# A hybrid decoder layer on one core: a new timetable for the mixer blocks, gates in two PSUM banks, an output projection begun early, and fewer query weight loads

## What is computed

```python
x <- LN1(alpha*x + Mixer(x)); x <- LN2(alpha*x + PEER(x))
Mixer: one input projection (1024 -> 2048), then
  group A (512): conv of 4 taps -> RG-LRU (two sigmoid gates, scan) -> * gelu(gate)
  group B (256): y = B * conv of 3 taps (C * x_sc)
  group C (256): softmax attention into 256 memory tokens (4 heads)
  RMSNorm of each group, then one output projection (1024 -> 1024)
PEER: q = x @ wq (16 sides of 128); scores against 128 keys a side; top 16 of the pair sums
  for each of 8 heads; for these 16 experts e of a head:
  out += softmax(score) * gelu(x . u[e]) * v[e]
```

## Time and profile before

| | |
|---|---|
| median of 3 runs | 3273.26 us (3269.31 to 3274.66) |
| the profiled execution | 3269.15 us |
| its span, first to last instruction | 3267.3 us |
| PE busy | 2525.7 us (77%) |
| DVE busy | 2146.8 us (66%) |
| ACT busy | 1432.7 us (44%) |
| POOL busy | 1235.9 us (38%) |
| moved by DMA | 1265.55 MB, mean 387 GB/s |
| of it the gathers (queue q0) | 1140.92 MB |
| granted clock of PE, mean | 0.844 |

### The profile page before, as it was taken

The page is one execution under the profiler, slowest core; times in us unless marked ns, Lnnn a source line. Parts: engine busy times, 40 slices in busy tenths (PEclk is TensorE's granted clock), DMA queues, the critical chain, the costliest instruction groups (busy, mean ns, idle before and its releaser), DMA issues.

```text
span 3267.3 us, 36242 instructions
## 1 busy us (share of the span) xinstructions
PE 2525.7 (77%) x10228; PEld 741.7 (23%) x10228; DVE 2146.8 (66%) x4901; ACT 1432.7 (44%) x4042; POOL 1235.9 (38%) x1092
## 2 busy tenths in 40 slices
PE   8889988789787898677887878876676766666675
PEld 4443432222111232122331112321111111110010
DVE  3545767878766567777767666556666666764554
ACT  3415545566434434456544334434444343443343
POOL 0014433344444344444334444343434343443342
PEclk9989998889898899799887988997767677777677
DMA  3449999899999999999989999999999999999997
GB/s 140 164 187 402 420 417 410 321 365 412 420 420 421 416 420 420 407 399 378 405 335 411 420 420 420 417 416 421 421 411 416 418 412 420 411 419 421 411 413 321
DMA packets 199720, 1265.55 MB, mean 387 GB/s; under 512 B 24160, under 2 KB 27488, under 8 KB 59616
## 3 DMA queue, kind: packets, MB, share of 16 engines
q0 software_dynamic: 156672, 1140.92, 85.1%
q1 hardware_dynamic: 42848, 122.32, 9.9%
HBM read 1245.49 MB, written 17.66 MB: 387 GB/s over the span
## 4 chain that ended last, share of the span: by engine, by line
issue 55%; POOL 33%; DMA 6%; PE 2%; DVE 2%; ACT 1%; POOLq 0%; SPq 0%; DVEq 0%; ACTq 0%
POOL arena L671 33%; DMA arena<-in_uv,idxT 5%; DVE arena L1525 1%; PE ps L940 1%; PE ps L698 1%; POOLq L663 0%; PE ps L720 0%; PE ps L924 0%; DMA arena<-in_w_in 0%; PE ps L889 0%; DVE bst L1485 0%; ACT wt L1130 0%; ACT wset L1135 0%; DVE bst L1383 0%; DVE arena L1393 0%
## 5 line engine op out<-in xcount | busy, mean ns | idle before, releaser
L671 POOL DMA_INDIRECT arena<-in_uv,idxT x1088 | 1235.7, 1136 | 2001.1 <-PE ps L940 1727.6
L940 PE MATMUL ps<-arena,wset 128*32 128x512 f32 x4352 | 1403.9, 746 | 659.4 <-ACT wset L1135 601.2
L1525 DVE CUSTOM_DVE_ANT_0 arena<-arena 128x1024 f32<-128x1024 f32 x1088 | 1329.9, 1224 | 838.8 <-DMA arena<-in_uv,idxT 798.6
L1126 ACT ACTIVATE gel<-acts 128x1 f32<-128x1 f32 x1088 | 219.8, 202 | 1403.8 <-DVE acts L1525 1402.1
L940 PEld LDWEIGHTS ps<-arena,wset 128*32 128x32 f32 x4352 | 176.9, 119 | 1600.2 <-ACT wset L1135 1394.1
L1130 ACT ACTIVATE wt<-gel,gT 128x1 f32<-128x1 f32 x1088 | 320.5, 295 | 102.5 <-ACT gel L1126 2.6
L1135 ACT ACTIVATE wset<-arena,wt 128x32 f32<-128x32 f32 x1088 | 349.5, 321 | 36.0
L698 PE MATMUL ps<-arena 128*128 128x384 f32 (+1 forms) x768 | 311.0, 524 | 28.7 <-DMA arena<-in_w_in 15.2
L859 PE MATMUL ps<-arena 128*128 128x128 f32 (+3 forms) x1024 | 294.8, 420 | 9.4 <-DMA arena<-in_wq 7.8
L924 PE MATMUL ps<-arena 32*128 32x512 f32 x704 | 243.8, 774 | 0.2 <-ACT arena L1108 0.2
L859 PEld LDWEIGHTS ps<-arena 128*128 128x128 f32 x1024 | 164.8, 194 | 208.4 <-issue 171.8
(11 more groups left out here) (171 smaller groups left out, 1514.1 us busy)
## 6 DMA issues: line engine op xcount, KB each, us to landing
arena<-in_wq SPq DMA_DIRECT2D x64, 512.0 KB
arena<-in_w_in SPq DMA_DIRECT2D x48, 512.0 KB
arena<-in_uv,idxT POOLq DMA_INDIRECT x1088
arena<-in_w_outs SPq DMA_DIRECT2D x16, 512.0 KB
arena<-scratch_q SPq DMA_DIRECT2D x30, 256.0 KB
arena<-in_x_tok SPq DMA_DIRECT2D x9, 512.0 KB, 8.1
scratch_x<-arena SPq DMA_DIRECT2D x9, 512.0 KB
arena<-in_w_out SPq DMA_DIRECT2D x1, 4096.0 KB, 13.6
```

What stands on the lines that cost most here:

```text
L671: pool.indirect_dma_start(out=ring[n % RING], out_offset=None, in_=A["uv"], in_offset=bass.IndirectOffsetOnAxis(ap=idxT[t % 2][:, col:col ...
L940: last = mm(ps[r0:r0 + 32, hf * HALF:(hf + 1) * HALF], wset[n % SETS][:, :], v[:, hf * HALF:(hf + 1) * HALF], start=first, stop=final)
L1126: A_(gel[:, n % COLS:n % COLS + 1], acts[:, n % COLS:n % COLS + 1], ACT.Gelu).then_inc(gelus, 1)
L1525: V.tensor_tensor_reduce(out=ring[n % RING][:, 0:D], in0=ring[n % RING][:, 0:D], in1=xrep[g % 2], scale=1.0, scalar=0.0, op0=ALU.mult, op1 ...
```

## The change

- BASE goes from [-200, 76, 384] to [-200, 72, 368]. In blocks 1 and 2 the order of input projections mixes groups A and B (`PROJ1`), a gate starts every 24 steps instead of 16 (`x = o + 16 + 24 * c`), both sigmoids stand on one step, "ra" is split in "ra" and "rc", attention rounds start at o + 18 + 16 r instead of o + 15 + 16 r, norms are spread, and the output projection starts at o + 140 (block 2: o + 150) instead of o + 142.
- Block 2's cache loads: "ss" and "sv" stand 8 steps apart instead of 1 or 3.
- In blocks 1 and 2 "gr" goes to the bank of the projection lx, "gi" to that of lg (`gbank`); norms' banks by `nbank`.
- Head: attention rounds every 3.5 steps instead of 4, the norm of G_MEM at 29 instead of 34, of G_LRU at 27 instead of 28. The two output halves of tile 0 are each split in "oa" (the 6 row blocks of G_LRU and G_MEM, which doesn't wait for G_SC; step 33) and "ob" (the other two; step 36).
- Sides 8 to 15 of block 0 are computed once for all 384 columns ("wa", steps 9 to 41, ACT copies tile 0's part to `qTb` and the rest to the store buffer); "wq" has only sides 0 to 7 left, from step 42. The order of the stores is k = 2, 3, 0, 1.
- First loads: xT is loaded in two halves with a semaphore each, before par and consts on SP; the first three weights, memT and wkv are issued by ACT.

```diff
-BASE = [LEAD, 76, 384]
+BASE = [LEAD, 72, 368]
+PROJ0 = [("qp", 0), ("qp", 1)] + LRU + SC
+PROJ1 = [("qp", 0), ("qp", 1)] + [x for c in range(3) for x in (LRU[2 * c], LRU[2 * c + 1], SC[c])] + LRU[6:] + SC[3:]
+PROJ = [PROJ0, PROJ1, PROJ1]
...
-        put("act", o + 8 * i + 6, b, name, c)
+        put("act", o + 8 * i + (6 if i < 14 else 7), b, name, c)
     for c in range(CL):
-        x = o + 16 * c
-        put("dve", x + 25, b, "cv", c)
-        put("pe", x + 31, b, "gr", c)
-        put("act", x + 31, b, "sr", c)
-        put("pe", x + 31.5, b, "gi", c)
-        put("act", x + 32, b, "si", c)
-        put("act", x + 33, b, "ta", c)
-        put("dve", x + 34, b, "ra", c)
-        put("act", x + 39, b, "sd", c)
-        put("dve", x + 40, b, "re", c)
-    for i in range(CS):
-        put("dve", o + 104.5 + 24 * i, b, "sh", i)
+        x = o + 16 + 24 * c
+        put("dve", x + 9, b, "cv", c)
+        put("pe", x + 15, b, "gr", c)
+        put("act", x + 15, b, "sr", c)
+        put("pe", x + 15, b, "gi", c)
+        put("act", x + 15, b, "si", c)
+        put("act", x + 16, b, "ta", c)
+        put("dve", x + 17, b, "ra", c)
+        put("dve", x + 20, b, "rc", c)
+        put("act", x + 23, b, "sd", c)
+        put("dve", x + 24, b, "re", c)
+    put("dve", o + 89, b, "sh", 0)
+    put("dve", o + 128, b, "sh", 1)
...
-        x = o + 15 + 16 * r
+        x = o + 18 + 16 * r
...
-            put("pe", o + 78 + i + 2 * (i // 2), b, "ss", i)
-            put("pe", o + 98 + i + 2 * (i // 2), b, "sv", i)
-        put("act", o + 85, b, "cs")
-        put("pe", o + 89, b, "sr4")
-        attend(ROUNDS[b], o + 89)
+            put("pe", o + 78 + 8 * i, b, "ss", i)
+            put("pe", o + 114 + 8 * i, b, "sv", i)
+        put("act", o + 104, b, "cs")
+        put("pe", o + 106, b, "sr4")
+        attend(ROUNDS[b], o + 106)
...
-    for g, x in ((G_LRU, 95), (G_MEM, 106), (G_SC, 134)):
+    for g, at, no in ((G_LRU, 115.5, 119), (G_MEM, 118 if b == 1 else 142, 124 if b == 1 else 145), (G_SC, 133, 136)):
...
-        x = 8 + 4 * r
+        x = 7 + 3.5 * r
...
-    for g, x in ((G_LRU, 28), (G_MEM, 34), (G_SC, 35)):
+    for g, x in ((G_LRU, 27), (G_MEM, 29), (G_SC, 35)):
...
-    for n, (ti, half) in enumerate(((0, 0), (0, 1), (1, 0))):
-        put("pe", v(36 + n), "op", (ti, half))
+    for arg in ((0, 0), (0, 1)):
+        put("pe", v(33), "oa", arg)
+        put("pe", v(36), "ob", arg)
+    put("pe", v(38), "op", (1, 0))
...
     for side in range(8, SIDES):
-        put("pe", 9 + 2 * (side - 8), "w0", side)
-        put("act", 9 + 2 * (side - 8) + 2, "w0", side)
-    plan_queries(0, 26, 3)
+        put("pe", 9 + 4 * (side - 8), "wa", side)
+        put("act", 9 + 4 * (side - 8) + 4, "wa", side)
+        if side % 4 == 3:
+            put("sp", 9 + 4 * (side - 8) + 5, "sq", side // 4)
+    plan_queries(0, 42, 3)
...
+    def pbank(b, name, c):
+        return MB[PROJ[b].index((name, c)) % 2]
+    def gbank(b, name, c):
+        return MB[1] if b == 0 else pbank(b, "lx" if name == "gr" else "lg", c)
+    def nbank(b, g):
+        return MB[1] if g == G_LRU or (b and g == G_SC) else MB[2]
+    def q_order(b, k):
+        return (k + 2) % 4 if b == 0 else k
...
-                load("xT", x8(zone1, b), A["xT"][:, :, t0:t0 + n_])
+                for i in range(2):
+                    ks = slice(i * KD // 2, (i + 1) * KD // 2)
+                    load(f"xT{i}", x8(zone1, b)[:, ks, :], A["xT"][:, ks, t0:t0 + n_])
...
+        mix(LEAD - 1)
+        load("par", par[:, :], A["par"])
         load("consts", consts[:, :], A["consts"])
-        load("par", par[:, :], A["par"])
-        mix(LEAD - 1)
-        load("memT", memT, A["memT"])
-        load("wkv", wkv, A["wkv"])
...
-                o_ = claim(MB[(2 * ti + half) % 3], "dve", b, "z", arg)
-                for k in range(KD):
+                ks = GROUPS[G_LRU][1] + GROUPS[G_MEM][1] + GROUPS[G_SC][1]
+                ks = {"op": ks, "oa": ks[:6], "ob": ks[6:]}[name]
+                k_ = MB[(2 * ti + half) % 3]
+                o_ = bank[k_] if name == "ob" else claim(k_, "dve", b, "z", arg)
+                if name == "oa":
+                    pe.wait_ge(ld["wout"], 16)
+                    after(pe, "dve", b, "no", G_LRU)
+                    after(pe, "dve", b, "no", G_MEM)
+                else:
+                    after(pe, "dve", b, "no", G_SC)
...
+        for i in range(WIN):
+            act.dma_start(win[i], A["w_in"][W_COL[PROJ0[i]]]).then_inc(ld_win[i], 16)
+        act.dma_start(memT, A["memT"]).then_inc(ld["memT"], 16)
+        act.dma_start(wkv, A["wkv"]).then_inc(ld["wkv"], 16)
```

More of the change, by code:

```diff
@@ L495, in parts, with last_query @@
         return buf[:, 0:halo + n_], s_
+    def pbank(b, name, c):
[6 more added lines that the diff above has]
+        return (k + 2) % 4 if b == 0 else k
     def q_stores(b, k):
         per_unit = [1, 1, 2]
-        before = sum(per_unit[b_] * 2 for b_ in range(b)) + per_unit[b] * (k // 2)
+        before = sum(per_unit[b_] * 2 for b_ in range(b)) + per_unit[b] * (q_order(b, k) // 2)
         return 16 * (before + per_unit[b])
+    def last_query(b):
+        return "wq", (SIDES // 2 if b == 0 else SIDES) - 1
     def quad(t, c):
@@ L605, in run @@
                 k, s_ = arg, stg[arg % 2]
-                after(sp, "act", b, "we", 4 * k + 3)
+                after(sp, "act", b, "wa" if b == 0 and k >= 2 else "we", 4 * k + 3)
                 t0, n_ = ((1, 2), (3, 3), (6, 2))[b]
@@ L801, in run @@
             elif name == "nm":
-                o_ = claim(MB[0 if arg == G_MEM else 1], "act", b, "rm", arg)
+                o_ = claim(nbank(b, arg), "act", b, "rm", arg)
                 ks = GROUPS[arg][1]
@@ L877, in keyscores @@
             if u < 4:
-                after(pe, "act", 0, "w0", 4 * u + 3)
+                after(pe, "act", 0, "w0" if u < 2 else "wa", 4 * u + 3)
             else:
@@ L974, in past_block @@
                 after(act, "dve", b - 1, "no", g)
-            for k in (2, 3):
-                act.wait_ge(st_q[k % 2], q_stores(b - 1, k))
+            for k in range(4):
+                if q_order(b - 1, k) >= 2:
+                    act.wait_ge(st_q[k % 2], q_stores(b - 1, k))
         def run(b, name, arg):
             n_, n0 = cols(b), BLOCKS[b][1]
-            bk = bank[MB[PROJ.index((name, arg)) % 2]] if (name, arg) in PROJ else None
-            if bk is not None:
+            if (name, arg) in IS_PROJ:
+                bk = bank[pbank(b, name, arg)]
                 after(act, "pe", b, name, arg)
@@ L1054, in run @@
                 after(act, "pe", b, "nm", arg)
-                ins = A_(rmsbuf[arg][:, 0:n_], bank[MB[0 if arg == G_MEM else 1]][:, 0:n_], ACT.Sqrt,
+                ins = A_(rmsbuf[arg][:, 0:n_], bank[nbank(b, arg)][:, 0:n_], ACT.Sqrt,
                          scale=1.0 / GROUPS[arg][2], bias=eps[:, 0:1])
@@ L1372, in run @@
                 if b == 0:
-                    after(dve, "pe", b, "op", arg)
+                    after(dve, "pe", b, "ob" if ti == 0 else "op", arg)
                 else:
```

121 lines of the change are left out of this document (63 added, 58 removed).

## The result

The changed kernel takes 3243.82 us (median of 4, 3243.0 to 3247.56) beside 3272.07 us for the kernel before on the same chip: a ratio of 0.9917, 95% interval 0.9901 to 0.9932. It is faster by 28 us, half of the 57 us forecast. Its profiled execution has a span of 3242.1 us (before: 3267.3).

The account below looks back on a forecast made before the run. The prediction took the kernel to be bound by its DMAs, above all the gathers, at 420 GB/s. Head -4, queries -7, SP wait +2, blocks -23 and -25 sum to -57 us: 3216 us, own range 3198 to 3234, outer 3191 to 3250.

Parts of the forecast that it names:

- The start: Head, first loads on two queues: consts lands after 3.5 MB, PE starts at 12.2 instead of 10.43 us, +1.8 us.
- the upper bound: Head's start: all 6.2 MB issued on ACT and SP there land before consts, first matmul at 19.5 us, +9.1 us.
- rival A: Head: ACT's loads go first, the start is 9.1 us late instead of 1.8; +7.3, total 3223 us; chance 0.27.
- The stretch between: Head, first matmul to last input projection: G_MEM's norm sum (1.5 us) moves ahead of that projection; no other cost.
- the cover: Head: G_LRU and G_MEM normed by the last projection's end, rounds packed for it; if not, up to 5.9 us lost.
- The output projection: Head, tile 0, last projection to transposes: 27.3 instead of 34.7 us, 7.4 less; with the norm sum's 1.5, 5.9 gained.
- Behind the transposes: Head, transposes to first gather: nothing changes, four first query sides and three outputs as before.
- Queries: Block 0, 255 to 461 us: sides 8 to 15's weights loaded once, 4.19 MB less; -7 us, between -3 and -10.
- The new wait on SP: Block 0: tile 1's query loads wait for late stores, PE may wait near step 80; +2 us, from 0 to +10.
- Blocks 1 and 2: Their gather stretches: spaced gates, rounds and cache loads recover bandwidth; -23 us (-10 to -31) and -25 (-12 to -33).
- Rival B: Blocks 1 and 2: losses come from in-order hand-overs, spacing halves them; -12 and -19, total 3233 to 3250; chance 0.20.
- Rival C: Blocks 1 and 2: PE's granted clock falls and PE becomes the bound; at 0.72 the kernel takes 3311 us; chance 0.05.

Follow-up runs that it names:

- e1: The changed kernel with consts and par issued ahead of xT on SP, ACT still issuing its loads: 3250.29 us, ratio 0.9922 to the kernel before.
- e4: The changed kernel with all first loads on SP, consts and par first, rounds still packed: 3242.60 us, ratio 0.9902 to the kernel before.
- e12: e10 with the head's attention rounds packed again at every 3.5 steps: 3230.92 us, ratio 0.9872 to the kernel before.
- e2: The changed kernel with the head's rounds every 4 steps again, G_LRU's norm at 28, G_MEM's at 32: 3246.67 us, ratio 0.9910 to the kernel before.
- e3: The changed kernel with the edits of both e1 and e2: 3241.38 us, ratio 0.9897 to the kernel before.
- e10: e5 with split output projection, G_MEM and G_SC norms at 32 and 33, first weights between xT's halves on SP: 3226.50 us, ratio 0.9848 to the kernel before.
- e5: The changed kernel with the head's loads, rounds, norms and output projection as before: 3228.22 us, ratio 0.9863 to the kernel before.
- e11: e5 with query weights of block 0's sides 8 to 15 read twice, as before: 3240.45 us, ratio 0.9896 to the kernel before.
- e7: The changed kernel with block 2's cache loads close together again: 3256.88 us, ratio 0.9950 to the kernel before.
- e8: The changed kernel with all gates in one bank, MB[1], again: 3258.78 us, ratio 0.9958 to the kernel before.
- e6: The kernel before with only the attention rounds of blocks 1 and 2 three steps later: 3343.07 us, ratio 1.0210 to the kernel before.
- e9: e6 with "ra" split, the gate's reciprocal three steps later as "rc": 3289.82 us, ratio 1.0047 to the kernel before.

## Why the gain was half of the forecast

**The start: wrong (+1.8 forecast, +8.9 measured).** The step that failed is "both queues move equal bytes, so consts lands when 3.5 MB have". It was the upper bound, rival A's: first matmul 19.5 by its working, 19.34 in the trace. e1 and e4 show that it is the pair of queues: xT, behind consts and par, lands 15.9 us after its issue beside ACT's loads (e1), and with the same order on one queue PE starts at 10.5 (e4). From 10 to 15 us the queues moved 1.84 and 0.27 MB, with 175 and 174 packets: equal turns, not equal bytes. This agrees with the Trainium skill (DMA: Bandwidth & Descriptors, "Queues, rings and completion order"), by which each DMA engine takes turns between the queues packet by packet. The prediction set ACT's descriptors at 4 KB, which holds for the weights; with memT and wkv the mean there was 10.5 KB. The row that I gave for it, xT beside the gathers at 29.4 us, was the right one, and I went by the middle of two bounds instead of by it.

**The stretch between: wrong, the largest miss (+1.5 forecast, +16.1 measured).** The 1.5 are G_MEM's norm sum, which the prediction moves ahead of the last projection. The prediction names the packing only as what pays for the cover ("the attention rounds are packed at 3.5 instead of 4 steps for that") and prices it at nothing; nor does its upper end for the head, +6, hold any of it. e12 shows 14.9 us of it by itself, e2 12.2 and e3 (beside e1) 16.8 once the norm sum is taken off. The rule to price it by was in the program: a round ties up a bank of PE until DVE has copied it, and that copy has its place in DVE's order behind the gate's work.

**The output projection: mechanism right, gain less (-5.9 forecast, -4.4 measured).** The term is -7.4 for the stage from the last projection to the transposes and +1.5 for the norm sum ahead of it; the stage gave -5.9. G_LRU and G_MEM were normed in time, and the wait for G_SC took 4.5 us where 5.0 were set. What was undersized are the two remainders: 3.5 us forecast, 6.2 measured (183.81 to 190.00), for behind the 4.50 us of idling PE had a granted clock of 0.50 (184 to 188 us). And the cover cost more than it hid, which no part of the sum asked. e10's stage is 4.0 us shorter than e5's without it.

**Behind the transposes: +2.2, forecast 0.** 36.9 against 34.7 us. PE waits 2.48 us for query weights (in_wq, at 204.69) where it waited 1.79 before, and the 32 matmuls behind it take 5.44 us instead of 3.93, at a granted clock of 0.65 and then 0.75 instead of 1.00: 0.7 + 1.5 = 2.2 us. e12, which waits 1.81 us there, takes 4.11 us and has 34.9; all others wait 2.5 to 3.4 us and have 36.9 to 37.8. Why the weights come later wasn't tested.

**Queries: not refuted (-7 forecast; with the wait on SP -5).** e11 gives -11, give or take 7, which holds the forecast as well as the -10.0 of the bytes alone; whether the discount for steps in which PE is the bound was needed can't be told. The new wait on SP was feared at +2 and cost nothing to be seen; SP's waits for stores, and the page's line of PE's wait for the queries, idle time last:

```profile
SPq L604 <- DMA scratch_q<-arena: 62.1, 4, 27.2
```
```profile
L921 PE MATMUL ps<-arena 128*128 128x128 f32 x256 | 42.6, 317 | 3.2 <-DMA arena<-scratch_q 2.8
```

SP waits longer at once (27.2 us against 19.0, rows 8), but PE only 2.8 us in all.

**Blocks 1 and 2: right in size (-23 and -25 forecast; -20.0 and -23.5 by the windows of this profile, -17 to -21 and -21 to -24 over the eight of the table).** The exp's wait of DVE in 560 to 760 us, 16.6 us in rows 7, is

```profile
DVE small L1370 <- ACT arena L1066: 2.3, 3, 1.4
```

and in_cv no longer stops PE in block 2. The mechanism was only partly the one that I told. Of the block 2 term, e7 gives 11 us, give or take 7, to the cache loads (forecast 13). The banks (e8) are worth 13 us, give or take 7, where I had them as a part of the rest. That rounds and gates must not share a step is not by itself what the gain rests on: e6 has them parted and loses 69 us, e9 loses 16. What is left is the gates' distance of 24 steps and what came with it (mixed projections, places of the norms, both sigmoids on one step). No run parts these, and the distance alone, on the kernel before, was not run: that it is the distance stays argued. The stretches between lost 2.7 and 6.9 us more than before (760 to 1340, 1720 to the end). The second is over the 5 us that I had named as a sign of being wrong, though a rounding of 1 GB/s is worth 3.6 us in so long a window. 255 to 461 also loses 6.4 us (1.5 before), which comes with the later first gather.

**The sum.** -57 forecast and -25.2 by the profiled spans: the head is 25.4 us worse than its term (start 7.1, packing 14.6, output 1.5, behind the transposes 2.2), the loop 6.5 worse. The measured 3244 lies inside the outer bounds, 3191 to 3250, but above the forecast's own range, 3198 to 3234. The rival that held in its cause was A, which would have given 3223; with the packing's price on it the sum comes to 3238, beside 3243.8. Rival B's band (hand-overs as such, 3233 to 3250) holds the measured 3244, but for a reason that the windows refute: the blocks gained what was forecast. Rival C did not come: the granted clock in the blocks is 0.95, 0.91 and 0.89. In the head, though, it did fall (0.90 and 0.96 instead of 1.00), where the prediction didn't look.

## What to carry to other kernels

Price a shorter spacing like an added operation: list who must have emptied which buffer before the next round may begin, and where that copy stands in the order of its engine. Small loads that the first instruction needs go first, and no second queue with larger descriptors starts beside them. When an operation is started early, look at what is queued behind it (here a norm sum of 1.5 us whose result the rest waits for); putting that ahead gave 4.0 us of that stage without buying anything else, though the whole kernel's gain from it is inside the error.

## What was not expected of the hardware

- 136 KB took 17.0 us to land while another queue had 4.72 MB in flight, and 3.7 us when issued 1.6 us earlier, ahead of xT (e1).
- PE's clock falls in the middle of a dense stretch: behind 4.39 us of idling eight matmuls took 5.11 us instead of 2.75, at a granted clock of 0.52. So a wait costs more than its length: in the head 8.3 us more of idling came with up to 6 us of slower work.
- Two queues side by side moved as many packets (175 and 174 in 5 us) and so very unequal bytes (1.84 and 0.27 MB).
- Moving the attention rounds of two blocks by three steps (some 9 us) cost 69 us, which nothing in the profile before had announced.
